# Seven half-size products for every second gate and up pair of a feed-forward network's long groups, with ScalarE copying the other pairs out of PSUM

## The reference

```python
def conv_ffn(xn, w_up, w_conv, w_down):          # first network, xn = rms_norm(h, g_ffn), 512 x 1024
    u = causal_depthwise_conv(xn @ w_up, w_conv) # 512 x 5632, each column a 3-tap filter over the tokens
    a, g = jnp.split(u, 2, axis=-1)
    return (a * jax.nn.silu(g)) @ w_down         # back to 512 x 1024

def swiglu(x, w_gate, w_up, w_down):             # second network
    return (jax.nn.silu(x @ w_gate) * (x @ w_up)) @ w_down
```

## Time and profile before

| | |
|---|---|
| median of 3 runs | 1371.1 us (1370.25 to 1371.47) |
| the profiled execution's own time | 1370.73 us |
| its span in the trace | 1368.9 us |
| TensorE busy | 1357.0 us, 99% |
| VectorE busy | 949.1 us, 69% |
| ScalarE busy | 607.7 us, 44% |
| granted TensorE clock, mean | 0.998 |

### The profile page before, as it was taken

How to read it: one execution, slowest core, us unless ns; L and a number is a source line. 1 busy time by engine, 2 the same in 40 slices (tenths; PEclk the granted TensorE clock), 3 DMA queues, 4 the chain that set the end, 5 groups by cost and what they waited for, 6 DMA issues and landing times.

```text
span 1368.9 us, 18308 instructions
## 1 busy us (share of the span) xinstructions
PE 1357.0 (99%) x6944; PEld 1134.3 (83%) x6944; DVE 949.1 (69%) x1302; ACT 607.7 (44%) x842; POOL 122.1 (9%) x143
## 2 busy tenths in 40 slices
PE   9999999999999999999999999999999999999997
PEld 7777886888788888888888888878888899989986
DVE  7767788555666755763676786777878689548944
ACT  6546686333444533431344554443344445325532
POOL 1010156000000000000000221014000000000000
PEclk9999999999999999999999999999999999999999
DMA  7222345421122332222321332341222332322321
GB/s 274 98 97 78 123 153 187 154 92 62 62 76 81 121 123 92 92 92 101 112 95 61 104 112 92 108 144 57 92 93 96 110 133 93 119 97 93 105 81 62
DMA packets 28160, 144.40 MB, mean 105 GB/s; under 512 B 3211, under 2 KB 8612, under 8 KB 13497
## 3 DMA queue, kind: packets, MB, share of 16 engines
q1 hardware_dynamic: 24744, 133.97, 28.7%
q0 software_dynamic: 2656, 8.72, 1.8%
q10 hardware_dynamic: 688, 0.73, 0.2%
HBM read 136.84 MB, written 6.30 MB: 105 GB/s over the span
## 4 chain that ended last, share of the span: by engine, by line
PE 94%; DVE 2%; ACT 1%; DMA 1%; issue 1%; SPq 0%; POOL 0%; DVEq 0%; ACTq 0%
PE ps L2127 28%; PE ps L2129 28%; PE ps L2128 28%; PE ps L2543 1%; PE ps L2345 1%; PE ps L2358 1%; PE ps L2493 1%; PE ps L2335 1%; PE ps L2384 1%; PE ps L2679 1%; PE ps L2681 1%; PE ps L2685 1%; PE ps L2386 0%; PE ps L2385 0%; DMA h<-x_t_dram 0%
## 5 line engine op out<-in xcount | busy, mean ns | idle before, releaser
L2127 PE MATMUL ps<-opA_hi,w_hi 128*128 128x512 f32 (+1 forms) x1008 | 385.0, 382 | 0.8 <-DVE w_lo L1302 0.4
L2129 PE MATMUL ps<-opA_hi,w_lo 128*128 128x512 f32 (+1 forms) x1008 | 380.9, 378 | 0.0
L2128 PE MATMUL ps<-opA_lo,w_hi 128*128 128x512 f32 (+1 forms) x1008 | 380.5, 378 | 0.0
L1302 DVE TENSOR_TENSOR w_lo<-raw,w_hi 128x2048 fp32r<-128x2048 f32 x112 | 256.6, 2291 | 87.1 <-ACT w_hi L727 85.7
L727 ACT CAST w_hi<-raw 128x2048 fp32r<-128x2048 f32 x111 | 211.6, 1907 | 233.2 <-PE ps L2129 232.9
L2127 PE MATMUL ps<-opB_hi,w_hi 128*128 128x512 f32 (+1 forms) x584 | 226.8, 388 | 1.7 <-DVE opB_lo L1338 1.0
L2129 PE MATMUL ps<-opB_hi,w_lo 128*128 128x512 f32 (+1 forms) x584 | 225.6, 386 | 0.0
L2128 PE MATMUL ps<-opB_lo,w_hi 128*128 128x512 f32 (+1 forms) x584 | 225.6, 386 | 0.0
L2127 PEld LDWEIGHTS ps<-opA_hi,w_hi 128*128 128x128 f32 x1008 | 189.8, 188 | 37.4 <-issue 1.9
L2129 PEld LDWEIGHTS ps<-opA_hi,w_lo 128*128 128x128 f32 x1008 | 189.7, 188 | 35.6
L2128 PEld LDWEIGHTS ps<-opA_lo,w_hi 128*128 128x128 f32 x1008 | 189.8, 188 | 34.0 <-issue 0.2
(11 more groups left out here) (452 smaller groups left out, 2027.9 us busy)
## 6 DMA issues: line engine op xcount, KB each, us to landing
raw<-weights_dram SPq DMA_DIRECT2D x113, 1024.0 KB, 4.9
g_dram<-g_stage POOLq DMA_DIRECT2D x8, 512.0 KB, 3.0
h<-x_t_dram SPq DMA_DIRECT2D x7, 512.0 KB, 7.2
g_spec<-g_dram SPq DMA_DIRECT2D x5, 512.0 KB, 3.4
...
```

The costliest lines, as they stand in the source:

```text
L1302: V.tensor_tensor(w_lo[:, p, :], raw[:, p, :], w_hi[:, p, :].bitcast(F32), ALU.subtract).then_inc(lo_ready, 1)
L2127: W.matmul(out, w[0], x[0], start=start, stop=False, skip_group_check=mixed)
L2128: W.matmul(out, w[0], x[1], start=False, stop=False, skip_group_check=mixed)
L2129: return W.matmul(out, w[1], x[0], start=False, stop=stop, skip_group_check=mixed)
```

## The change

The first network's two long groups, `up1_0` and `up1_1`, are done by seven products in every second pair.

- A list `PAIRS_1` gives each pair a kind. **C**: as before (the six pairs of `up1_2`). **W**: the even pairs of `up1_0` and `up1_1` (40, 42, ..., 58; eight in all), by seven products. **V**: the odd ones, by the plain products, but now on normalised tokens. **D**: pairs of `w_down`.
- As the operand of both groups is now normalised tokens, VectorE makes `x_norm` (eight instructions after pairs 30 and 31), `t_sum` (after pair 32), its low parts (after pair 33) and the low half of the new `opA` (in pairs 36 and 37); ScalarE makes the high parts.
- In V pairs VectorE no longer empties PSUM: ScalarE copies each chunk to `z_pad` and makes the third tap straight from PSUM.
- In W pairs VectorE adds the products up into `z_pad` and makes the weight sums; ScalarE copies one more half bank.
- GpSimd's clearing of `nyq`, `first_one`, `ones_r` and `acc_next` moves to the start of pair 60, as `nyq` shares its place with `t_hi`.
- The loops of the first network are written out. The second network's code becomes shared functions, with two of its three `s_sum` instructions made one of 128x1024, and two of its products exchanged in order of use of the sums.

```diff
+        PAIRS_1 = []
+        for n, g in enumerate(FFN_ORDER):
+            for i in range(FFN_GROUPS[g]):
+                PAIRS_1.append((FIRST[f"up1_{g}"] + i, "C" if n == 0 else "V" if i % 2 else "W", i, FFN_COUNT[g] + i))
+            if g != FFN_LAST:
+                PAIRS_1 += [(FIRST[f"down1_{g}"] + i, "D", i, 0) for i in range(4)]
...
-            pool.wait_ge(pv_done, 40)
+            pool.wait_ge(chunk_done, 2 * FIRST[f"down1_{FFN_LAST}"])
...
+            def keep_product(net, g, n, kept):
+                if g in net.count:
+                    act.wait_ge(*past(net.m_done, 6 * net.count[g] + n))
+                    A.copy(kept[g % 2][:], ps[:, 4 * (g % 2) + (0, 0, 0, 2, 3)[n], 0:HALF]).then_inc(net.m_copied[0], 1)
...
+            def first_net_pair(g, kind, i, n):
+                p, net = g % 2, FIRST_NET
+                z = z_pad[:, p, :, 2:2 + T]
+                def tap(j, source):
+                    A.activation(conv[:, p, j, :], source, ACT.Copy, scale=vec("ffconv", 2 * 2 * FT + j * FT + tile)).then_inc(tapped, 1)
+                if kind != "D":
+                    tile = 8 * [x for x in FFN_ORDER if FIRST[f"up1_{x}"] <= g < FIRST[f"down1_{x}"]][0] + i
+                if kind == "C":
+                    pair_hi(net, g + 2)
+                    for j in range(2):
+                        act.wait_ge(bank_read, 2 * g + j + 1)
+                        tap(j, z[:, j, :])
+                elif kind == "V":
+                    keep_product(net, g + 1, 1, m1)
+                    for j in range(2):
+                        act.wait_ge(chunk_done, 2 * g + j + 1)
+                        A.copy(z[:, j, :], ps[:, 4 * p + j, :])
+                        tap(j, ps[:, 4 * p + j, :])
+                    pair_hi(net, g + 2)
+                elif kind == "W":
+                    act.wait_ge(*past(net.m_done, 6 * net.count[g] + 5))
+                    A.copy(z[:, 0, 0:HALF], ps[:, 4 * p, 0:HALF]).then_inc(z_copied, 1)
+                    pair_hi(net, g + 2)
+                    act.wait_ge(z_copied, Z_COPIED_BASE + net.count[g] + 1)
+                    act.wait_ge(z_made, Z_BASE + net.count[g] + 1)
+                    for j in range(2):
+                        tap(j, z[:, j, :])
+                else:
+                    if i < 2 and g < FIRST[f"up1_{FFN_ORDER[1]}"]:
+                        operand_hi(net, i, 2 * FIRST[f"down1_{FFN_ORDER[0]}"])
+                    pair_hi(net, g + 2)
+                sums_hi(net, g + 2)
+                if kind != "V":
+                    keep_product(net, g + 1, 1, m1)
+                keep_product(net, g + 1, 3, m5)
+                keep_product(net, g + 1, 4, m6)
+                if kind != "D":
+                    act.wait_ge(conved, n + 1)
+                    A.activation(conv[:, p, 1, :], conv[:, p, 1, :], ACT.Silu).then_inc(gated, 1)
+                    act.wait_ge(act_prod, n + 1)
+                    A.copy(op_hi[1][:, i, :], conv[:, p, 0, :]).then_inc(act_hi, 1)
+                if kind == "C" and i == 2:
+                    token_sums_hi(net)
...
+            def sums(net, g):
+                if g in net.count:
+                    p, k = g % 2, net.count[g]
+                    dve.wait_ge(*past(net.s1_made, k + 1))
+                    for other in net.count:
+                        if other < g and other % 2 == p and (other in (g - 2, g - 4) or net.count[other] == k - 1):
+                            dve.wait_ge(chunk_done, 2 * other + 2)
+                    S.link(V.tensor_tensor(s_sum[p][:, 0, :], quarter(raw, p, 1, 0), quarter(raw, p, 0, 0), ALU.subtract))
+                    late = raw[:, p, :].rearrange("p (j half n) -> p j half n", j=2, half=2)[:, :, 1, :]
+                    V.tensor_tensor(s_sum[p][:, 1:3, :], late, s_sum[p][:, 0, :].unsqueeze(1).to_broadcast([P, 2, T]), ALU.subtract
+                                    ).then_inc(net.s_made[0], 1)
...
+            def first_net_pair(g, kind, i, n):
+                p, net = g % 2, FIRST_NET
+                z = z_pad[:, p, :, 2:2 + T]
+                if kind == "D":
+                    for j in range(2):
+                        product(2 * g + j)
+                        V.tensor_tensor(h[:, 2 * i + j, :], ps[:, 2 * p + j, :], h[:, 2 * i + j, :], ALU.add).then_inc(bank_read, 1)
+                    if i < 2 and g < FIRST[f"up1_{FFN_ORDER[1]}"]:
+                        operand_lo(net, i)
+                    sums(net, g + 2)
+                    split_pair(g + 2)
+                    sums_lo(net, g + 2)
+                    s1(net, g + 3)
+                    if i == 3:
+                        dve.wait_ge(bank_read, 2 * g + 2)
+                    return
+                tile = 8 * [x for x in FFN_ORDER if FIRST[f"up1_{x}"] <= g < FIRST[f"down1_{x}"]][0] + i
+                if kind == "C":
+                    for j in range(2):
+                        product(2 * g + j)
+                        V.tensor_tensor(z[:, j, :], ps[:, 2 * p + j, :], rstd[:], ALU.mult).then_inc(bank_read, 1)
+                elif kind == "W":
+                    add_products(net, g, z[:, 0, :], z[:, 1, :], None, z_made)
+                sums(net, g + 2)
+                split_pair(g + 2)
+                if kind == "C":
+                    dve.wait_ge(bank_read, 2 * g + 2)
+                dve.wait_ge(tapped, 2 * n + 2)
+                if kind == "W":
+                    dve.wait_ge(z_made, Z_BASE + net.count[g] + 1)
+                if kind != "C":
+                    V.engine_nop().then_inc(bank_read, 2)
+                for j in (1, 0):
+                    for tap in (1, 0):
+                        ins = V.scalar_tensor_tensor(conv[:, p, j, :], z_pad[:, p, j, tap:tap + T],
+                                                     vec("ffconv", tap * 2 * FT + j * FT + tile), conv[:, p, j, :], ALU.mult, ALU.add)
+                        if j == 1 and tap == 0:
+                            ins.then_inc(conved, 1)
+                        else:
+                            S.link(ins)
+                dve.wait_ge(gated, n + 1)
+                V.tensor_tensor(conv[:, p, 0, :], conv[:, p, 0, :], conv[:, p, 1, :], ALU.mult).then_inc(act_prod, 1)
+                sums_lo(net, g + 2)
+                s1(net, g + 3)
+                dve.wait_ge(act_hi, n + 1)
+                lo_part(op_lo[1][:, i, :], conv[:, p, 0, :], op_hi[1][:, i, :]).then_inc(act_lo, 1)
+                if kind == "C":
+                    if i < 2:
+                        normalised(net, range(4 * i, 4 * i + 4))
+                    elif i == 2:
+                        token_sums(net)
+                    elif i == 3:
+                        token_sums_lo(net)
+            for pair in PAIRS_1:
+                first_net_pair(*pair)
...
+            def long_group(net, group):
+                section = f"up{1 + (net.name == 'ffn2')}_{group}"
+                if group == FFN_ORDER[1]:
+                    pe.wait_ge(*past(net.tx_lo_made, 8))
+                for i in range(8):
+                    g = FIRST[section] + i
+                    if g in net.count:
+                        by_halves(net, g, i)
+                        continue
+                    pair_ready(g)
+                    pe.wait_ge(bank_read, 2 * g - 2)
+                    for j in range(2):
+                        chunk(g % 2, j, X[0], ps[:, 4 * (g % 2) + j, :]).then_inc(chunk_done, 1)
             for n, g in enumerate(FFN_ORDER):
-                gemm(f"up1_{g}", X[0], operand=None if n else next_lo, count=16, norms=() if n else [(1, 2)])
+                if n:
+                    long_group(FIRST_NET, g)
+                else:
+                    gemm(f"up1_{g}", X[0], operand=next_lo, count=16, norms=[(1, 2)])
```

More of the change, by code:

```diff
@@ new lines, in normalised, with token_sums @@
+            def normalised(net, ks):
+                for k in ks:
+                    S.link(V.scalar_tensor_tensor(x_norm[:, k, :], h[:, k, :], vec(net.gain, k), rstd[:], ALU.mult, ALU.mult))
+            def token_sums(net):
+                b11, b12, b21, b22 = (x_norm[:, 4 * r:4 * r + 4, c * HALF:(c + 1) * HALF] for r in range(2) for c in range(2))
+                for t, one, other in ((0, b12, b11), (1, b22, t_sum[:, 0]), (2, b22, b12), (3, t_sum[:, 1], b21)):
+                    V.tensor_tensor(t_sum[:, t], one, other, ALU.subtract).then_inc(net.t_made[0], 1)
+                    dve.wait_ge(*past(net.t_made, t + 1))
@@ new lines, in token_sums_lo, with operand_lo @@
+            def token_sums_lo(net):
+                for t in range(4):
+                    dve.wait_ge(*past(net.t_hi_made, t + 1))
+                    lo_part(t_lo[:, t], t_sum[:, t], t_hi[:, t]).then_inc(net.tx_lo_made[0], 1)
+            def operand_lo(net, i):
+                for k in range(2 * i, 2 * i + 2):
+                    dve.wait_ge(*past(net.x_hi_made, k + 1))
+                    lo_part(op_lo[0][:, 2 * k:2 * k + 2, :], x_norm[:, 2 * k:2 * k + 2, :], op_hi[0][:, 2 * k:2 * k + 2, :]
```

(1 more changed line is left out.)

301 lines of the change are left out of this document (104 added, 197 removed).

## The result

The changed kernel takes **1376.38 us** (median of 6 runs, 1376.23 to 1377.08), the kernel before in the same comparison 1370.62 (1370.21 to 1371.47). The ratio is 1.0042, 95% interval 1.0032 to 1.0053: 5.8 us more, where 14.8 were forecast. The profiled execution's span is 1374.5 us, 5.6 more than before.

The account below looks back on a forecast made before the run. TensorE, busy 99% of the span, was taken to set the time unless another engine is late. 1370.7 + 11.9 (token operand) - 6.7 (seven products) + 9.6 (ring through both engines) = 1385.5 us; own range 1381.5 to 1390, wider 1375.5 to 1391.

Parts of the forecast that it names:

- price 2: In the long groups, a dependency loop through VectorE and ScalarE outlasts TensorE's two pairs: +9.6 us, including delays behind the groups.
- price 1: In `up1_2`, making the token operand adds 15.8 us to VectorE, so TensorE starts pair 40 late: +11.9 us.
- the gain: In the long groups, eight W pairs of seven products take TensorE 10.04 us each, not 10.88: 6.7 us less.
- the first rival: In the long groups, V-to-V timing costs TensorE nothing; only the token operand costs: 1376 us; chance 0.13 for 1374 to 1381.5.
- only these 5.5 us can take up work: In `up1_2`, of VectorE's waits only those for `w_hi`, taps and TensorE, 5.5 us, can absorb work put between pairs.
- The 1.7 for ScalarE's `t_hi`: In `up1_2`, a new VectorE wait: ScalarE makes four `t_hi` before `w_hi` of pair 35, 1.7 us.
- the sign that price 1 falls: No TensorE wait ahead of pair 36 would show the forecast +11.9 us for the token operand wrong.
- the ring takes 23.2 us: From one V pair's `w_lo` to the next, VectorE 18.1 plus ScalarE 5.1 us, against TensorE's 20.92; ends 22.6 to 23.8.
- the prediction's own rule: Each long group has two turns between V pairs; the first has 0.8 us slack, the second none: 3.8 us lost a group.
- The ring has slack: In the long groups, the V-to-V loop costs nothing, leaving +11.9 and -6.7: 1376 us; chance 0.13 for 1374 to 1381.5.
- The clock drops in the new waits: TensorE's waits around pair 35 halve its clock; up to 8.2 us more per pair if lasting into 36 to 39; chance 0.12.
- The token operand hides: In `up1_2`, VectorE has 16 us of room for making the operand, so the kernel ends near 1364 us; chance 0.05.

Follow-up runs that it names:

- kernel 4: The changed kernel with ScalarE's `w_hi` in V pairs moved ahead of the two copies and two taps from PSUM: 1374.57 us, ratio 1.0027.
- experiment 1: The kernel before with only its first network written out pair by pair, no token operand and no seven products: 1370.77 us, ratio 0.9999.
- experiment 10: The changed kernel with ScalarE's four `t_hi` moved into pairs 33 and 34, VectorE's `t_lo` behind pair 34: 1374.79 us, ratio 1.0029.
- kernel 5: The changed kernel with two unread VectorE multiplications (1.2 us together) added at the end of each V pair: 1383.97 us, ratio 1.0096.
- kernels 2: The changed kernel without its seven products: token operand made and used, every pair of the long groups a V pair: 1380.62 us, ratio 1.0069.
- Kernels 4 and 9: 9: the changed kernel with the operand's making spread over VectorE's waits and later pairs, and `w_hi` first in V pairs: 1368.25 us, ratio 0.9982.
- kernel 11: The spread operand with `w_hi` first in V pairs, plus the last two `t_lo` behind pair 39's additions to `h`: 1365.36 us, ratio 0.9963.

## Why the prediction was right in kind and wrong in size

Forecast were 11.9 - 6.7 + 9.6 = 14.8 us, measured are 9.4 - 6.2 + 2.3 = 5.5 in the traces. The direction was right; of the 9.3 us between the two, 7.3 are price 2, 2.5 price 1, and 0.5 the gain, the other way. 1376.4 lies below the prediction's own range of 1381.5 to 1390; only the wider one of 1375.5 to 1391, which takes in the first rival, holds it.

- **The gain of TensorE, -6.7: nearly right.** By kernel 4, where nothing else stands in the groups, it is 2 x 3.1 = 6.2; a W pair takes 10.07 and a V pair 10.91. The 256-column matmul stayed near the rows' 119.6 ns.
- **Price 1, +11.9: the mechanism right, the size 9.4.** The step that failed is "only these 5.5 us can take up work". With the loops written out the room is 8.1 (experiment 1), and the last `opB_lo` without the operand at 488.54. The prediction's own sum then gives 488.54 + 15.8 - 8.1 + 1.6 = 497.8 for the last `opB_lo`, 8.5 later than before; it started at 498.03, 8.7 later. `w_lo` of pair 38 adds 0.75 (forecast 0.6), which makes the 9.4. The 1.7 for ScalarE's `t_hi` was right (experiment 10: 1.6). The waits lay on `w_lo` of 35 and 38 and on `opB_lo`, as forecast, but there was none ahead of pair 36, which the prediction had named as the sign that price 1 falls. It didn't fall, and the sign was a bad one: TensorE was at half pace in pair 35. At full pace it would have been through at 472.49 + 10.88 = 483.4, and `w_lo` of 36 was ready at 485.3; the wait of 1.9 was run as slow matmuls. In kernel 5, with 7 of them for 14, there is a wait ahead of pair 36, of 0.17 us.
- **Price 2, +9.6: the mechanism right, the size some 2.3.** The step that failed is "the ring takes 23.2 us". It takes 21.94, outside the 22.6 to 23.8 given. VectorE's and ScalarE's rows of the changed kernel, start to start, against the prediction's terms: the taps 3.03 for 3.3, twice, 0.5 less; product to `opB_lo` 1.38 for 1.60, 0.2 less; five additions and sums 3.90 for 4.11, and product to `opB_hi` 0.72 for 0.82, 0.3 less; ScalarE's part 4.85 for 5.1, 0.25 less. None is large; together they are 1.3 us, 5% of the ring, and more than half of the 2.3 by which it was to exceed TensorE. With an excess of 0.96 and the 0.8 of slack in the first turn the prediction's own rule gives 0.16 + 0.96 = 1.1 a group, and 1.07 was lost. The prediction named the taps' registers, at 0.05 a tap, and put them in the range and not in the sum. At 23.13 (experiment 5) the forecast price came out to within 0.3 us a group.
- **The rivals.** "The ring has slack", 1376, has the right time by luck: it takes 11.9 for price 1 and nothing for the ring, where 9.4 and 2.3 were measured, and the two misses cancel. "The clock drops in the new waits" happened, and as written there "in a stretch where VectorE is the later one", so it had no price of its own in the changed kernel (kernels 2 and 5, above). Kernels 4 and 9 show the other case, with TensorE the later one: 0.7 and 1.5 us. "The token operand hides", 1364, fell for this code, but kernel 11, where the operand is spread, comes within 1.4 us of it. Of what was to show it, the waits before pair 40 sum to 5.7 us and not 11, the stalls are 1.0 us in pairs 46 and 58 and 0.1 in 44 and 56, none in the pairs named as free, and VectorE's wait ahead of a V pair's `w_lo` is 2.6 for 2.9.

Both misses have one main cause: all of the added room in `up1_2`, and 0.9 of the ring's 1.3 us. VectorE's durations were taken from the loops of before and applied to code that is written out, and they were used in two places where small differences are multiplied: six pairs without room, and a ring whose length is compared with another.
